# The delta rule's triangular inverse from 8 by 8 blocks, with the blocks' product and substitution behind level five's first parts

## The reference

```python
a_mat = jnp.where(strict, jnp.einsum('bnhid,bnhjd->bnhij', kb, kc) * decay, 0.0)
unit_lower = a_mat + jnp.eye(C, dtype=a_mat.dtype)
u = solve(unit_lower, vb)
w = solve(unit_lower, kb * jnp.exp(gc)[..., None])
...
v_new = u_i - jnp.einsum('bhcd,bhde->bhce', w_i, state)
o = (jnp.einsum('bhcd,bhde->bhce', q_i * jnp.exp(g_i)[..., None], state)
     + jnp.einsum('bhij,bhje->bhie', qk_i, v_new))
```

## Time and profile before

| | us |
|---|---|
| runs, median of 3 | 2768.18 |
| runs, lowest and highest | 2764.29, 2771.28 |
| the profiled execution | 2771.26 |
| its span in the profile | 2769.4 |
| PE busy | 2725.2 (98%) |
| DVE busy | 1542.8 (56%) |
| ACT busy | 1312.0 (47%) |
| POOL busy | 119.9 (4%) |

### The profile page before, as it was taken

One profiled execution on the slowest core, in us unless ns is written; L12 is line 12 of the kernel. 1 busy time (PEld: TensorE's weight loads), 2 busy tenths in 40 slices (PEclk: granted clock), 3 DMA queues, 4 the chain that ended last, 5 costly groups with the idle time before them and its releaser, 6 DMA issues.

```text
span 2769.4 us, 44546 instructions
## 1 busy us (share of the span) xinstructions
PE 2725.2 (98%) x18174; PEld 2393.0 (86%) x18174; DVE 1542.8 (56%) x2048; ACT 1312.0 (47%) x1798; POOL 119.9 (4%) x167
## 2 busy tenths in 40 slices
PE   8999999999999999999999999999999999999999
PEld 8999998888888888888898997888888888888887
DVE  5655466666555555555544665666665555455454
ACT  4544444555544535445444354335555444354453
POOL 0000043000000000000000000530000000000000
PEclk9999999999999999999999999999999999999999
DMA  7454500543555555555545562004445545555553
GB/s 281 181 184 159 182 33 32 213 172 143 184 201 184 190 191 189 190 183 186 193 175 201 188 220 95 2 2 160 175 140 195 192 173 197 183 191 191 183 194 140
DMA packets 67801, 461.71 MB, mean 167 GB/s; under 512 B 7023, under 2 KB 10223, under 8 KB 13084
## 3 DMA queue, kind: packets, MB, share of 16 engines
q1 hardware_dynamic: 63824, 449.47, 45.3%
q10 hardware_dynamic: 3500, 5.21, 0.6%
q0 software_dynamic: 288, 4.19, 0.4%
HBM read 456.73 MB, written 5.27 MB: 167 GB/s over the span
## 4 chain that ended last, share of the span: by engine, by line
PE 94%; DVE 3%; ACT 2%; issue 1%; DMA 0%; POOL 0%; DVEq 0%; ACTq 0%; POOLq 0%
PE bank L423 17%; PE bank L402 13%; PE bank L404 13%; PE bank L403 13%; PE bank L425 9%; PE bank L446 6%; PE bank L448 6%; PE bank L447 6%; PE bank L1199 1%; PE bank L1172 1%; PE bank L337 1%; PE bank L2477 1%; PE bank L561 0%; PE bank L505 0%; DVE split_lo L353 0%
## 5 line engine op out<-in xcount | busy, mean ns | idle before, releaser
L353 DVE TENSOR_TENSOR split_lo<-raw,split_hi 128x1024 fp32r<-128x1024 f32 x840 | 1019.9, 1224 | 943.1 <-ACT split_hi L346 942.7
L346 ACT ACTIVATE split_hi<-raw 128x1024 fp32r<-128x1024 f32 x840 | 881.4, 1059 | 1137.6 <-PE bank L404 554.9
L423 PE MATMUL bank<-hT,split_hi 128*128 128x512 f32 x2048 | 720.8, 397 | 5.4 <-issue 5.3
L425 PE MATMUL bank<-hT,split_lo 128*128 128x256 f32 x2048 | 574.4, 280 | 0.0
L423 PEld LDWEIGHTS bank<-hT,split_hi 128*128 128x128 f32 x2048 | 385.0, 188 | 93.4 <-DVE split_lo L353 1.1
L402 PE MATMUL bank<-split_hi,u_hi 128*128 128x512 f32 x1152 | 449.8, 390 | 0.0
L404 PE MATMUL bank<-split_hi,u_lo 128*128 128x512 f32 x1152 | 448.5, 389 | 0.0
L403 PE MATMUL bank<-split_lo,u_hi 128*128 128x512 f32 x1152 | 448.4, 389 | 0.0
L425 PEld LDWEIGHTS bank<-hT,split_lo 128*128 128x128 f32 x2048 | 387.4, 189 | 5.7 <-issue 5.6
L446 PE MATMUL bank<-hT,split_hi 128*128 128x256 f32 x1328 | 376.8, 284 | 0.0
L448 PE MATMUL bank<-hT,split_lo 128*128 128x256 f32 x1328 | 375.8, 283 | 0.0
(11 more groups left out here) (471 smaller groups left out, 2266.4 us busy)
## 6 DMA issues: line engine op xcount, KB each, us to landing
raw<-in_stream SPq DMA_DIRECT2D x420, 1024.0 KB, 4.8
work<-in_mem POOLq DMA_DIRECT2D x2, 2048.0 KB, 8.5
bias_rows<-bias_line SPq DMA_DIRECT2D x1, 3072.0 KB, 12.9
x<-in_x SPq DMA_DIRECT2D x1, 2048.0 KB, 9.0
out<-x SPq DMA_DIRECT2D x4, 512.0 KB, 4.9
mwork<-bias_rows ACTq DMA_DIRECT2D x1, 1536.0 KB, 11.2
work<-bias_rows ACTq DMA_DIRECT2D x1, 1536.0 KB, 10.1
rwork<-in_wide ACTq DMA_DIRECT2D x1, 1280.0 KB, 5.9
```

Source lines behind the costliest of these rows:

```text
L346: nc.scalar.activation(split_hi[:, u % SPLIT], raw[:, b % RAW, (u % 2) * UNIT:(u % 2 + 1) * UNIT], ACT.Copy).then_inc(s_hi, 1)
L353: nc.vector.tensor_tensor(split_lo[:, u % SPLIT], raw[:, b % RAW, (u % 2) * UNIT:(u % 2 + 1) * UNIT], f32(split_hi[:, u % SPLIT]), SUB).th ...
L423: nc.tensor.matmul(out[:, :], lhsT=w_hi[:, cols], rhs=hT[:, k].rearrange("p two s -> p (two s)"), start=k == 0, stop=False)
L425: m = nc.tensor.matmul(out[:, S:2 * S], lhsT=w_lo[:, cols], rhs=hT_hi[:, k, :], start=False, stop=k == KD - 1)
```

## The change

In groups 0 to 3 (the delta rule) the inversion starts from the inverses of 8x8 diagonal blocks and runs levels 3 to 6 alone; groups 4 to 7 keep levels 0 to 6. The 8x8 inverses come from three new pieces. `dve_inv_blocks` cuts the blocks out of `iv_diag`, sums them into a compact form and spreads them over 64 columns. `pe_inv_around` is one product with a block matrix, 128x128 by 512 columns, which gives all eight rows of a block to each of its partitions. `dve_inv_solve` does the forward substitution by rows on DVE, with a wait between any two steps, and spreads and transposes the result.

The slot tables are new, since a group has 16 slots on PE and 8 on ACT and DVE. The product stands at PE's slot 10, behind the second product of level five's direction 0; the substitution stands on DVE at slot 4, behind level five's direction 0, and so ahead of its direction 1. The blocks stand on DVE behind level four's direction 0. The cum, mask and kk products of a group's direction 0 stand at the end of the group two before it (for group 1 ahead of group 0), with ACT's exponentials. In the head, AT comes ahead of QKT, the product stands behind unit 6 of the last chunk and the substitution ahead of `take_output`. The fillers at slots 20 and 23 go; group 0 has 14 filler products at slots 4 and 8, groups 2 and 3 have 8 at slot 15. The squares go to ACT, with a sum each, but for the last group's. POOL makes the values in three parts behind three waits, and its scaled queries wait for the last tail step of two groups before. The output product's units inside group 3 are three, at slots 5 to 7. The masks of levels 0 to 2, which only layer 1 uses now, come by a DMA of their own during the window stage. The first product of a group waits for level six of the group before.

```diff
+BASE = 3
+TINY = 1 << BASE
...
-    ("ident", P), ("level", 2 * (LEVELS - 1) * (P // 2)), ("eye", P // 2),
+    ("ident", P), ("level", 2 * (LEVELS - 1 - BASE) * (P // 2)), ("eye", P // 2),
+    ("blocks", P // 2), ("around", P), ("unit", TINY), ("unit_neg", 1),
     ("neg", 2 * P), ("cum_mid", 4 * P), ("causal", 4 * P), ("halves", P), ("ones", 1), ("half_cols", 2),
     ("pick", 16),
 ]
+LOW_COLS = 2 * BASE * (P // 2)
...
+        def base_of(group):
+
+            return BASE if group < 4 else 1
...
-                pe.wait_ge(iv_t, nth(group, level - 1, d))
+                if level == base_of(group):
+                    pe.wait_ge(iv_tt, iv_tt_first(group, d))
+                    if group % 4:
+                        pe.wait_ge(iv_t, nth(group - 1, MASKS, d))
+                else:
+                    pe.wait_ge(iv_t, nth(group, level - 1, d))
...
+        def rep_bank(group):
+            return bank[6 if group else 4]
+
+        def dve_inv_blocks(dve, group, views, d):
+
+            T, Tt = views[0][:, d], views[1][:, d]
+            if group >= 2 and d == 0:
+                dve.wait_ge(iv_f, group - 1)
+            dve.wait_ge(iv_a, 2 * group + d + 1)
+            own = const[:, C["blocks"]].unsqueeze(1).broadcast_to([P, 4, HALF])
+            dve_step(nc.vector.tensor_tensor(Tt, iv_diag[:, d], own, MULT))
+            dve_step(nc.vector.reduce_sum(tiny[:, 0, d], blocks_of(Tt).rearrange("p m b c -> p m c b"), AX_X))
+            unit = const[:, C["unit"]].unsqueeze(1)
+            unit = unit.unsqueeze(2) if d else unit.unsqueeze(3)
+            got = tiny[:, 0, d].unsqueeze(3) if d else tiny[:, 0, d].unsqueeze(2)
+            shape = [P, 4, TINY, TINY]
+            nc.vector.tensor_tensor(blocks_of(T), got.broadcast_to(shape), unit.broadcast_to(shape), MULT).then_inc(iv_blk, 1)
+
+        def pe_inv_around(pe, group, views):
+
+            pe.wait_ge(iv_blk, 2 * group + 2)
+            pe.wait_ge(s_eg, 2 * group + 2)
+            nc.tensor.matmul(rep_bank(group)[:, :], lhsT=const[:, C["around"]],
+                             rhs=views[0].rearrange("p d m n -> p (d m n)"), start=True, stop=True).then_inc(iv_rep, 1)
+
+        def dve_inv_solve(dve, group, views):
+
+            T, Tt = views[0], views[1]
+            N = rep_bank(group)[:, :].rearrange("p (q k c) -> p q k c", k=TINY, c=TINY)
+            row = tiny[:, 1].rearrange("p d m c -> p (d m) c")
+            part = tiny[:, 2].rearrange("p d m c -> p (d m) c")
+            unit = const[:, C["unit"]].unsqueeze(1).broadcast_to([P, 8, TINY])
+            dve.wait_ge(iv_rep, group + 1)
+            nc.vector.tensor_copy(row[:, :, 0:1], unit[:, :, 0:1])
+            dve_step(nc.vector.scalar_tensor_tensor(out=row[:, :, 1:], in0=N[:, :, 0, 1:], scalar=const[:, C["unit_neg"]],
+                                                    in1=unit[:, :, 1:], op0=MULT, op1=ADD))
+            for k in range(1, TINY - 1):
+                left = TINY - 1 - k
+                dve_step(nc.vector.tensor_tensor(part[:, :, 0:left], N[:, :, k, k + 1:],
+                                                 row[:, :, k:k + 1].broadcast_to([P, 8, left]), MULT))
+                dve_step(nc.vector.tensor_tensor(row[:, :, k + 1:], row[:, :, k + 1:], part[:, :, 0:left], SUB))
+            own = const[:, C["blocks"]].rearrange("p (b c) -> p b c", c=TINY).unsqueeze(1).broadcast_to([P, 4, TINY, TINY])
+            flat = lambda v: v.rearrange("p m s -> p (m s)")
+            for d, (solved, turned) in enumerate(((Tt, T), (T, Tt))):
+                nc.vector.tensor_tensor(blocks_of(solved[:, d]), own, tiny[:, 1, d].unsqueeze(2).broadcast_to([P, 4, TINY, TINY]),
+                                        MULT).then_inc(iv_tt, 1)
+                dve.wait_ge(iv_tt, 8 * group + 2 * d + 1)
+                nc.vector.transpose(flat(turned[:, d]), flat(solved[:, d])).then_inc(iv_tt, 1)
...
+            for piece in ("cum", "mask", "kk"):
+                pe_delta_pre(pe, 1, 0, piece)
             for hp in range(DN_GROUPS):
                 def between(slot):
                     for step in range(5):
                         if hp and slot == DN_PE["tail"][step]:
                             pe_delta_tail(pe, hp - 1, step)
+                    if hp == 0 and slot in (4, 8):
+                        pe_fill(bank[0], 14)
+                    if hp + 1 < DN_GROUPS and slot == DN_PE["around"]:
+                        pe_inv_around(pe, hp + 1, dn_inv[(hp + 1) % 2])
+                    if hp >= 2 and slot == 15:
+                        pe_fill(bank[1], 8)
                     for d in range(2):
                         for piece in PIECES[d]:
-                            if hp + 1 < DN_GROUPS and slot == DN_PE[piece][d]:
-                                pe_delta_pre(pe, hp + 1, d, piece)
-                    if slot in (20, 23):
-                        pe.wait_ge(s_D, min(2 * hp + 4, 2 * DN_GROUPS))
-                        pe_fill(bank[7], 4 if slot == 20 else 5)
+                            its = hp + (2 if DN_PE[piece][d] == 15 else 1)
+                            if its < DN_GROUPS and slot == DN_PE[piece][d]:
+                                pe_delta_pre(pe, its, d, piece)
 
                 pe_inv(pe, hp, dn_inv[hp % 2], [dn_AT[hp % 2][:, d] for d in range(2)], between)
...
-        DN_PE = {'tail': (0, 1, 3, 7, 9), 'cum': (0, 13), 'mask': (2, 13), 'kk': (0,), 'kq': (10,)}
-        DN_ACT = {'tail': (0, 1, 3), 'pre': (1, 7), 'diag': (9, 11)}
-        DN_DVE = {'R': 1, 'out': 3, 'squares': 5, 'QKT': (5, 8), 'AT': (7, 9), 'first': (9, 11)}
+        DN_PE = {'tail': (0, 2, 4, 7, 11), 'cum': (15, 2), 'mask': (15, 2), 'kk': (15,), 'kq': (6,), 'around': 10}
+        DN_ACT = {'tail': (0, 1, 3), 'pre': (7, 1), 'diag': (1, 2), 'squares': 4}
+        DN_DVE = {'AT': (0, 1), 'blocks': (2, 2), 'R': 1, 'solve': 4, 'out': 6, 'QKT': (6, 7)}
...
+            elif (c, u) == (5, 6):
+                pe_inv_around(pe, 0, dn_inv[0])
...
-                pe.wait_ge(s_AT, 2 * hp)
+                pe.wait_ge(s_AT, 4 * hp - (2 if piece == "kk" else 0))
             elif hp == 1 and d == 0:
-                pe.wait_ge(s_AT, 2)
+                pe.wait_ge(s_AT, 4)
+                pe.wait_ge(iv_tt, 1)
+            elif hp and d == 0:
+                pe.wait_ge(s_eg, 2 * hp)
+                pe.wait_ge(iv_tt, 8 * (hp - 1) + 1)
             elif hp:
                 pe.wait_ge(s_eg if piece == "cum" else s_D, 2 * hp + d)
...
+            act_delta_pre(act, 1, 0)
             for hp in range(DN_GROUPS):
                 def between(slot):
                     for step in range(3):
                         if hp and slot == DN_ACT["tail"][step]:
                             act_delta_tail(act, hp - 1, (step,))
                     for d in range(2):
-                        if hp + 1 < DN_GROUPS and slot == DN_ACT["pre"][d]:
-                            act_delta_pre(act, hp + 1, d)
+                        its = hp + (2 if DN_ACT["pre"][d] == 7 else 1)
+                        if its < DN_GROUPS and slot == DN_ACT["pre"][d]:
+                            act_delta_pre(act, its, d)
                         if hp + 1 < DN_GROUPS and slot == DN_ACT["diag"][d]:
                             act_delta_diag(act, hp + 1, d)
-                    if hp + 1 == DN_GROUPS and 7 <= slot < 7 + AHEAD:
+                    if hp >= 2 and slot == DN_ACT["squares"]:
+                        act_delta_squares(act, hp - 2)
+                    if hp + 1 == DN_GROUPS and slot >= 5:
                         act.wait_ge(s_o, DN_GROUPS - 1)
-                        hi_upto(act, starts["ev_out"][1] + slot - 6)
+                        hi_upto(act, starts["ev_out"][1] + slot - 4)
+                    if hp + 1 == DN_GROUPS and slot == 7:
+                        act_delta_squares(act, hp - 1)
...
                 lo_sc(5, 1 + d)
-                dve_delta_QKT(dve, 0, d)
+                dve_delta_AT(dve, 0, d)
             for d in range(2):
                 lo_sc(5, 3 + d)
-                dve_delta_AT(dve, 0, d)
+                dve_delta_blocks(dve, 0, d)
             for d in range(2):
-                dve_inv_first(dve, 0, dn_inv[0], d)
+                dve_delta_QKT(dve, 0, d)
+            dve_inv_solve(dve, 0, dn_inv[0])
             take_output(5)
...
             for hp in range(DN_GROUPS):
                 def between(slot):
+                    for d in range(2):
+                        if hp + 1 < DN_GROUPS and slot == DN_DVE["AT"][d]:
+                            dve_delta_AT(dve, hp + 1, d)
+                        if hp + 1 < DN_GROUPS and slot == DN_DVE["blocks"][d]:
+                            dve_delta_blocks(dve, hp + 1, d)
                     if hp and slot == DN_DVE["R"]:
                         dve_delta_R(dve, hp - 1)
+                    if hp + 1 < DN_GROUPS and slot == DN_DVE["solve"]:
+                        dve_inv_solve(dve, hp + 1, dn_inv[(hp + 1) % 2])
                     if hp and slot == DN_DVE["out"]:
```

(50 more changed lines are left out.)

155 lines of the change are left out of this document (93 added, 62 removed).

## The result

The changed kernel takes 2781.8 us (median of 7 runs, 2779.1 to 2789.08), the kernel before 2771.28 on the same chips (7 runs): 1.0047 of the time, 95% interval 1.0035 to 1.0058, so 10 to 16 us slower. The forecast was 2765.3, 2.9 faster. The profiled execution of after has a span of 2787.1, 7 us over the median of this kernel's runs (2779.9). It shows three things at once, which have to be told apart.

A forecast was written before the change was run, and what follows sets the result against it. PE held 94% of the chain, its delta rule stage bound by the number of small PE instructions. Terms summed to -6.2 us at full clock, +3.3 for a clock fall: -2.9, so 2765.3 us against 2768.18, range 2757 to 2773.

The forecast's parts named there:

- Prices: Unit costs: substitution 4.7 us on DVE, blocks 3.0 for both directions (bounds 2.6 and 3.9), around product 0.9 on PE.
- Head, +5.1: Convolution's end to group 0: around product, substitution and output delay group 0's start from 360.69 to 365.8, with 0.6 and 1.7 waits.
- Rival (2): Two or three clock falls, the head's two waits causing one: 2768.6 to 2771.9 us; chance 0.24, shared with longer steps.
- longer steps: DVE's substitution steps exceed 0.22 us: each 0.1 more costs +4.8; at 0.30, 2769.1 us; chance 0.24, shared with Rival (2).
- Group 0, +3.7: Delta rule's first group: 25.0 us against 21.33, with PE idle 3.9 us for the substitution.
- Groups 1 and 2, -10.0: Delta rule's middle groups: 23.8 us each against 28.8, with PE waits of 0.9 and 1.1 us.
- rival (3): Clock falls in every group behind 0.9 and 1.1 us waits, fillers gone; five falls give 2778.5 us; chance 0.07.
- Group 3, -5.1: Delta rule's fourth group, without blocks or substitution: 21.3 us against 26.41.
- POOL's cover, costed at nothing: Delta rule: POOL's later mask levels still end before level four reads them; otherwise 2.8 us of mask products join the path.
- Output product, +0.1: Behind group 3: one unit fewer is split ahead of the output product, 0.1 us more.
- Elsewhere, 0: Outside the stage: the extra mask DMA from ACT (bounds 0 and 0.35 us) and layer 1's recurrence cost nothing.
- The clock, +3.3: One fall of 7 us at half speed behind group 0's 3.9 us idle: +3.3 us, bounds 1.8 and 3.7.

The follow-up runs named there:

- a_cover: The changed kernel with filler products added in PE's waits in the delta rule (head, groups 0 to 2): 0.9976 of before.
- a_minus20: The changed kernel with 5 filler products fewer (20 PE instructions) behind level six of group 3: 1.0028 of before.
- a_wait40: The changed kernel with 80 waits on a set semaphore (40 instructions) ahead of PE's first product: 1.0003 of before.
- a_cover_late: a_cover with the substitution one DVE slot later, behind level five's direction 1, and group 0's filler moved behind level six, 10 products for 16: 1.0003 of before.
- best: a_cover_late with 48 more waits on a set semaphore (24 instructions) ahead of PE's first product: 0.9978 of before.
- best_head: best with group 1's cum, mask and kk products behind group 0's first level product, and 16 fillers during the substitution wait: 0.9977 of before.
- best_addr256: best_head with an unused SBUF tile of 224 bytes a partition, so the tiles behind it stand 256 bytes on from before: 0.9972 of before, 2759.72 us.

## Why the prediction was wrong

In the prediction's order, against the trace of after where nothing else is said.

**Prices.** The substitution was right: steps 0.21 to 0.24 apart, 4.7 us from its copy to its end, for groups 1 to 3. In the head it took 5.2, with two steps of 0.50 and 0.44, both with two SBUF inputs and beside POOL's work from 362.9 to 364.3; the steps between them, with one operand in PSUM, kept 0.17. The blocks were mis-sized: 3.15 us for groups 2 and 3, but 4.4 in the head and 4.6 for group 1, which group 0 makes, above my upper bound of 3.9. The head's first direction on DVE:

```profile
353.06 0.64 DVE L1303 TENSOR_REDUCE tiny<-work 128x32 f32<-128x256 f32 x1
353.73 0.88 DVE L1308 TENSOR_TENSOR work<-tiny,const 128x256 f32<-128x256 f32 x1
```

The reduce takes 0.61 to 0.65 and not the 0.39 of the earlier trace rows, whose output is 4 columns wide where this one's is 32. And the spreads pay the price of L1238 while POOL runs: in the head and in group 0 six of eight take 0.86 to 0.95, two 0.42 and 0.64. That is the rule of the Trainium skill that the prediction cites (SBUF — State Buffer, "Who interferes with whom"), and the trace agrees in the main: the second spread takes 0.42 to 0.43 for the first direction of groups 2 and 3, beside which POOL has nothing, and one 0.42 stands in the head where POOL had started. My bound had this price for the spreads and failed by the reduce. The around product took 1.07 (I took 0.9).

**Head, +5.1: it was 7.5** (0.85 for the around product and 6.6 behind the convolution). 1.4 us of blocks too many, and a unit of 1.76 us beside POOL, made QKT end at 360.75 and the substitution start there, 2 us later than worked out. With the half clock behind them these gave the 7.5; in a_cover, whose head has no fall, it was 6.6.

```profile
364.91 0.56 PE L1590 MATMUL bank<-rowsT,pick 128*128 128x256 f32 x2 [2.08 <-issue]
...
367.39 2.05 PE L1599 MATMUL bank<-work 128*128 128x128 f32 x8 [1.06 <-DVE work L1888]
```

The two waits are the 0.6 and the 1.7 of the prediction, at 2.08 and 1.06. Rival (2) named the two together as enough for a fall, and it came, so that the kk behind them takes 2.05 us and not 1.09. But it came at 365.1, 0.2 us behind the first wait and ahead of the second: here the first alone was enough, the one that I had at 0.6. In a_minus20 (365.8) and a_wait40 (367.7) the fall came in or behind the second. No row spoke against that rival; I had given it, with longer steps, one case in four.

**Group 0, +3.7: right at full clock, +6.8 as run.** The wait of 3.9 us was 3.88:

```profile
391.95 0.72 PE L1223 MATMUL bank<-work,mwork 64*64 64x64 f32 x8 [3.88 <-DVE work L1358]
```

In a_cover, without a fall in this group, it took 25.2 us (25.0 predicted). The fall at 392.4 came as forecast; the one of the head reached into the group's first 2.5 us as well.

**Groups 1 and 2, -10.0: -5.7.** Group 2, at full clock, took 24.60 us (23.8 predicted): its waits were 0.22, 1.34 and 0.69 in place of 0.1, 0.9 and 1.1, the around product 0.2 more; 0.5 I can't name. Group 1 took 27.34 with the end of one fall and the whole of another, behind a wait of 1.34 for level four's direction 1. The same wait in group 2 cost none, and in a_minus20 it cost none in either group; in before, group 3 has a wait of 1.21 us that cost none. What I held against rival (3), "0.95 us waits cost none", was true, but the waits were not of 0.95, and neither their length nor the rows of before tell which of them costs a fall.

**Group 3, -5.1: -5.3**, with 0.45 us behind the squares (0.9 predicted) and 1.47 behind the output units (1.4). POOL's cover, costed at nothing, held: no product waited for a mask. **Output product, +0.1: +0.5. Elsewhere, 0:** right for ACT's DMA and layer 1's recurrence (its clock falls differ from run to run, 1.3 us in after's favour), and wrong by its largest term: 6.2 us of stalls and the half clock behind them in layer 1's MLP. No step of mine looked at the length of PE's program, though the chain of before showed "issue 1%" and the stall itself stood in the earlier trace rows as the longest gap of the trace. I used it to price the clock and didn't ask what it was.

**The clock, +3.3.** Three falls and not one. At full clock the change gives about -3 us by rows free of falls (head 6.6 in a_cover with around, group 0 3.9, group 1 -4.7 by a_cover's 25.84 less half of its 3.4 us fall, group 2 -4.2, group 3 -5.3, output 0.5), against my -6.2, so 3 us of the error are sizes, 1.5 of them in the head, 1.1 in groups 1 and 2, most of it DVE's blocks and what waits behind them (argued from the rows, not tested by a run); the measured +3.8 leaves 7 us to the clock, 3.7 more than forecast. Each size is from one execution. The rest, 5 to 9 us, is the placement, which none of the rivals held. So the step that failed by most is "Elsewhere, 0": the change of the program's length was costed at nothing and brought 5 to 9 us through the stalls at the loop's turns. The next is the clock, one fall forecast and three measured (3.7 us), and then the blocks.

## What to carry to other kernels

Ahead of a change to the length of a program with loops, look for waits of PE behind issue at the turns: if there are any, shift the program by a few idle instructions and measure that first, and compare every variant at a place without stalls. Products removed from PE's path are not a gain where their removal opens a wait: price the half clock behind each new wait, several short ones within a few microseconds included, and keep or add filler there. A stage with short waits has to be compared by its falls of the clock first: the stages of 118.43 and 110.83 us differ by 7.6 us, and the first holds 20.4 us at half clock where the second holds none. The substitution's later slot gained 1.35 us in group 0, but only some 0.4 to 0.9 in all (an estimate from a_cover, a_cover_late and best), since the waits moved to later groups.

## What the runs showed that I had not expected

- 40 instructions more in idle time make this kernel 6 to 9 us faster (0.9968 and 0.9980), with 154 loads of instructions in place of 157; 20 make it 9 us slower. The stall at a turn is 3.6 to 3.9 us less what PE has left of the block.
- Fillers of 2.4 us a group shorten groups 1 and 2 by 1.7 us: 28.8 us with, 30.5 without, PE's clock over the stage being 1.00 with them and 0.89 without.
- A product pair of the MLP takes 346.7 or 353.3 ns for a whole turn; moving the tiles by 32 bytes decides which, for the first turn, with two exceptions in the 34 first turns of 17 traces, both in layer 1 with the tiles 32 bytes on. Why, and what decides for the later turns, is open.
- A reduce to 32 columns takes 0.62 us where one to 4 columns from as many inputs takes 0.39.
- The same waits cost the clock in one execution and not in another: the stage of a_cover_late and best_head took 110.8 us without a fall, that of best and best_addr256 113.8 and 114.0 with two each.
